# A linear-attention mix: two score levels copied by another engine, more projection products between the scores, and an earlier begin

## The reference

```python
log_a = jax.nn.log_sigmoid(g_in @ w_up + b_up) / 16        # per key channel
# per chunk and head, G = cumsum(log_a)
o_inter = einsum('tk,kv->tv', q_ * exp(G), S)
A[t, s] = sum_k q_[t, k] * k_[s, k] * exp(G[t, k] - G[s, k])   for s <= t
o = o_inter + A @ v_
S = exp(G_last)[..., None] * S + (k_ * exp(G_last - G)).T @ v_
```

## Time and profile before

| | us |
|---|---|
| median of 3 runs | 2460.87 |
| lowest and highest run | 2460.1, 2465.82 |
| span of the profiled execution | 2455.2 |
| TensorE busy | 2293.2 (93%) |
| VectorE, ScalarE, POOL busy | 1172.6, 876.3, 902.2 |

### The profile page before, as it was taken

The page is one execution under the profiler, slowest core; times in us unless marked ns, Lnnn a source line. Parts: engine busy times, 40 slices in busy tenths (PEclk is TensorE's granted clock), DMA queues, the critical chain, the costliest instruction groups (busy, mean ns, idle before and its releaser), DMA issues.

```text
span 2455.2 us, 35075 instructions
## 1 busy us (share of the span) xinstructions
PE 2293.2 (93%) x14164; PEld 1750.4 (71%) x14164; DVE 1172.6 (48%) x2262; ACT 876.3 (36%) x1444; POOL 902.2 (37%) x962
## 2 busy tenths in 40 slices
PE   7988999999999999879999889999999999998898
PEld 7866878986695876545697678789857859664456
DVE  4278243525336127666333881446162452277662
ACT  4332124714334334333333222156143244333341
POOL 2255112215525410555422642122345263115552
PEclk9989999999999999989999999999999999999899
DMA  4100232230100113100321003312301002131003
GB/s 151 56 19 1 87 107 87 70 137 1 35 18 1 50 56 120 60 1 1 138 70 56 19 2 98 121 61 95 112 1 35 18 1 69 37 137 43 1 1 129
DMA packets 92016, 141.28 MB, mean 58 GB/s; under 512 B 18352, under 2 KB 65488, under 8 KB 91856
## 3 DMA queue, kind: packets, MB, share of 16 engines
q1 hardware_dynamic: 91856, 139.05, 16.6%
HBM read 105.48 MB, written 33.55 MB: 57 GB/s over the span
## 4 chain that ended last, share of the span: by engine, by line
PE 79%; DVE 14%; ACT 2%; issue 2%; POOL 2%; DMA 0%; SPq 0%; POOLq 0%; DVEq 0%; ACTq 0%
PE psum L240 37%; PE psum L504 12%; PE psum L1392 5%; PE psum L1354 3%; DVE gla_A L766 3%; PE psum L1375 3%; PE psum L1340 3%; PE psum L1378 3%; PE psum L1380 3%; PE psum L745 2%; PE psum L1399 1%; PE psum L997 1%; POOL w_lo L198 1%; PE psum L1778 1%; PE psum L882 1%
## 5 line engine op out<-in xcount | busy, mean ns | idle before, releaser
L198 POOL TENSOR_TENSOR w_lo<-w_raw,w_hi 128x512 fp32r<-128x512 f32 (+3 forms) x240 | 322.1, 1374 | 823.6 <-ACT w_hi L189 823.6
L240 PE MATMUL psum<-h_hi,w_hi 128*128 128x512 f32 x768 | 200.8, 404 | 0.0
L240 PE MATMUL psum<-h_lo,w_hi 128*128 128x512 f32 x768 | 199.1, 403 | 0.0
L1587 POOL TENSOR_TENSOR mla_acc<-mla_acc,mla_p 128x512 f32<-128x512 f32 (+3 forms) x160 | 159.7, 1015 | 103.1 <-ACT mla_p L1446 103.1
L240 PE MATMUL psum<-h_hi,w_lo 128*128 128x512 f32 x768 | 192.2, 392 | 0.0
L240 PE MATMUL psum<-w_hi,h_hi 128*128 128x256 f32 (+3 forms) x1280 | 183.7, 286 | 0.0
L240 PE MATMUL psum<-w_hi,h_lo 128*128 128x256 f32 (+3 forms) x1280 | 179.6, 283 | 0.0
L240 PE MATMUL psum<-w_lo,h_hi 128*128 128x256 f32 (+3 forms) x1280 | 179.4, 283 | 0.0
L1587 POOL TENSOR_TENSOR fox_acc<-fox_acc,fox_p 128x512 f32<-128x512 f32 (+3 forms) x160 | 149.9, 958 | 75.5 <-ACT fox_p L1446 75.4
L189 ACT ACTIVATE w_hi<-w_raw 128x2048 fp32r<-128x2048 f32 (+3 forms) x60 | 113.6, 1893 | 175.1 <-PE psum L504 169.8
L240 PEld LDWEIGHTS psum<-h_lo,w_hi 128*128 128x128 f32 x768 | 147.7, 195 | 32.1
(11 more groups left out here) (324 smaller groups left out, 4428.8 us busy)
## 6 DMA issues: line engine op xcount, KB each, us to landing
w_raw<-in_w_in_dram SPq DMA_DIRECT2D x38, 1024.0 KB, 5.3
out_dram<-x_rows SPq DMA_DIRECT2D x64, 512.0 KB, 2.7
x_rows<-out_dram SPq DMA_DIRECT2D x56, 512.0 KB, 5.2
w_raw<-in_w_out_dram SPq DMA_DIRECT2D x16, 1024.0 KB, 6.5
x_first<-in_x_dram SPq DMA_DIRECT2D x8, 512.0 KB, 7.0
x_rows<-in_x_dram SPq DMA_DIRECT2D x8, 512.0 KB, 6.0
w_raw<-in_w_in_dram SPq DMA_DIRECT2D x2, 1088.0 KB, 8.7
w_raw<-in_w_in_dram SPq DMA_DIRECT2D x2, 1056.0 KB, 5.2
```

The costliest lines, as they stand in the source:

```text
L198: last = pool.tensor_tensor(self.w_lo[c["set"]][:, at], self.w_raw[c["set"]][:, at], self.w_hi[c["set"]][:, at].bitcast(F32), ALU.subtract)
L240: last = pe.matmul(o, lhs, rhs, start=(kk == 0 and n == 0), stop=(kk == KT - 1 and n == 2))
L1587: pool.tensor_tensor(acc, acc, p, ALU.add).then_inc(self.acc_done.sem, 1)
```

## The change

Three things. (1) In every tile levels 1 and 2 of A are no longer predicated copies of VectorE but plain copies of ScalarE (move_level: one for level 1, on 64 partitions, two for level 2, on 32 each), placed between decay and square; the next batch's scores, finish and the next tile wait for their signal (moved). (2) The slots hold ten matmuls each, 240 in all, which are the two k units of the second half of the positions and the eight dx units, cut where they fall. The mix begins behind the two k units of the first half; tile 4 waits for the others. z stands one unit earlier, ScalarE takes the logs before the third q unit, makes the decays of tile 0 behind the first k unit, and rounds dx0 behind the second. (3) POOL splits dx1 and gA0 by quarters, behind batch 1 and behind the end of tiles 2, 3 and 6, 7.

```diff
     def split_chunk(self, pool, layer, name):
+        for i in range(4):
+            self.split_quarter(pool, layer, name, i)
+    def split_quarter(self, pool, layer, name, i):
         j = self.chunk_of[layer, name]
...
         n = self.chunk_size(c)
-        pool.wait_ge(self.w_rounded, j + 1)
-        for i in range(4):
-            at = slice(i * n // 4, (i + 1) * n // 4)
-            last = pool.tensor_tensor(self.w_lo[c["set"]][:, at], self.w_raw[c["set"]][:, at],
-                                      self.w_hi[c["set"]][:, at].bitcast(F32), ALU.subtract)
-        last.then_inc(self.w_split, 1)
+        if i == 0:
+            pool.wait_ge(self.w_rounded, j + 1)
+        at = slice(i * n // 4, (i + 1) * n // 4)
+        last = pool.tensor_tensor(self.w_lo[c["set"]][:, at], self.w_raw[c["set"]][:, at],
+                                  self.w_hi[c["set"]][:, at].bitcast(F32), ALU.subtract)
+        if i == 3:
+            last.then_inc(self.w_split, 1)
...
     def product(self, pe, layer, name, n, *part):
+        self.product_part(pe, layer, name, n, 0, KT, *part)
+    def product_part(self, pe, layer, name, n, first_kk, end_kk, *part):
...
         w_hi, w_lo = (w[c["set"]][:, :KT * width].rearrange("p (k n) -> p k n", n=width) for w in (self.w_hi, self.w_lo))
-        if n == 0:
+        if n == 0 and first_kk == 0:
             self.wait_bank(pe, u)
-        if n == 0 and first:
+        if n == 0 and first_kk == 0 and first:
             pe.wait_ge(self.w_rounded, j + 1)
...
         w, h = ((w_hi, self.h_hi), (w_hi, self.h_lo), (w_lo, self.h_hi))[n]
-        for kk in range(KT):
+        for kk in range(first_kk, end_kk):
             if c["kind"] == "C":
...
             last = pe.matmul(o, lhs, rhs, start=(kk == 0 and n == 0), stop=(kk == KT - 1 and n == 2))
-        if n == 2:
+        if n == 2 and end_kk == KT:
             last.then_inc(self.unit_done, 1)
...
 C_PARTS = [(m, n) for m in range(2) for n in range(2)]
+BY_HALF = [(m, n) for n in range(2) for m in range(2)]
 OUT_GROUPS = [(h, n) for h in range(2) for n in range(2)]
...
     chunk("q", "C", C_AQ, CHUNK, 0)
-    chunk("k", "C", C_AK, CHUNK, 1)
+    k.add_chunk(layer, "k", "C", C_AK, CHUNK, 1)
+    for part in BY_HALF[:2]:
+        k.add_unit(layer, "k", part, "act")
     k.ring, k.turn = (2, 3), 0
+    for part in BY_HALF[2:]:
+        k.add_unit(layer, "k", part, "act")
     chunk("dx0", "C", C_DX, CHUNK, 0)
...
     IN, END = LEVELS, LEVELS + 1
-    OPS = 1 + LEVELS
+    PLAIN = 2
+    OPS = 1 + LEVELS - PLAIN
     BATCHES = ((1, 2), (3, 4, 5), (6, 7))
...
              "gla_mean": TT, "gla_rstd": TT, "gla_normed": TT, "y_turned": self.GROUPS, "y_ready": self.GROUPS,
-             "end_decays": 1}
+             "end_decays": 1, "gla_moved": TT * self.PLAIN}
         (self.loaded, self.masks_loaded, self.a_turned, self.a_copied, self.z_done, self.z_biased, self.logs, self.exponents,
...
          self.out_done, self.state_product, self.state_new, self.squares, self.mean, self.rstd_ready, self.normed,
-         self.y_turned, self.y_ready, self.end_decays) = (Signal(k, name, count) for name, count in n.items())
+         self.y_turned, self.y_ready, self.end_decays, self.moved) = (Signal(k, name, count) for name, count in n.items())
...
-    def chunk_pool(self, pool, c):
-        if c == 0:
-            self.k.evacuated(pool, self.layer, "k", 1, 1)
+    def chunk_pool(self, pool, c, between):
+        if c in (0, TT // 2):
+            self.k.evacuated(pool, self.layer, "k", 1, 2 * c // TT)
         pool.wait_ge(self.decays.sem, self.decays.at(c + 1))
...
             last.then_inc(self.products.sem, 1)
+            if b == 1:
+                between(pool)
         for slot, src in ((self.IN, self.qT), (self.END, self.kT)):
...
         last.then_inc(self.chunk_ends.sem, 1)
+        between(pool)
...
         if c == 0 and b == 0:
-            self.k.evacuated(pe, self.layer, "k", 1, 1)
+            self.k.evacuated(pe, self.layer, "k", 1, 0)
             pe.wait_ge(self.z_biased.sem, self.z_biased.at(GN * self.N16))
...
             pe.wait_ge(self.masked.sem, self.masked.at(self.OPS * c))
+            pe.wait_ge(self.moved.sem, self.moved.at(self.PLAIN * c))
+            if c == TT // 2:
+                self.k.evacuated(pe, self.layer, "k", 1, 1)
+        elif b == 1:
+            pe.wait_ge(self.moved.sem, self.moved.at(self.PLAIN * (c + 1)))
         else:
-            pe.wait_ge(self.masked.sem, self.masked.at(self.OPS * c + self.BATCHES[b][0]))
+            pe.wait_ge(self.masked.sem, self.masked.at(self.OPS * c + self.BATCHES[b][0] - self.PLAIN))
         if b == 0:
...
         for x, level in enumerate(self.BATCHES[b]):
+            if level <= self.PLAIN:
+                continue
             B = self.HALF >> (level - 1)
-            dve.wait_ge(self.masked.sem, self.masked.at(n0 + level))
+            dve.wait_ge(self.masked.sem, self.masked.at(n0 + level - self.PLAIN))
             ps = self.scores_at(b, x, self.HALF).rearrange("p i g (n b) -> p (i g) n b", b=B)
...
+    def move_level(self, act, c, level):
+        if level == 1:
+            act.wait_ge(self.masked.sem, self.masked.at(self.OPS * c + 1))
+        B = self.HALF >> (level - 1)
+        ps = self.scores_at(0, level - 1, self.HALF).rearrange("p i g x -> p (i g) x")
+        for n in range(self.HALF // B):
+            r, first = slice(2 * B * n, 2 * B * n + B), 2 * B * n + B
+            last = act.activation(self.A[r, :, first:first + B], ps[r, :, B * n:B * n + B], ACT.Copy)
+        last.then_inc(self.moved.sem, 1)
...
             self.decay(act, c + 1)
+        self.move_level(act, c, 1)
+        self.move_level(act, c, 2)
         if c >= 1:
...
         pe.wait_ge(self.masked.sem, self.masked.at(self.OPS * (c + 1)))
+        pe.wait_ge(self.moved.sem, self.moved.at(self.PLAIN * (c + 1)))
         for g in range(GN):
...
             gla.turn_a(pe)
-        if i == 2:
+        if i == 1:
             gla.z(pe)
-    for part in C_PARTS:
+    for part in BY_HALF[:2]:
         k.project(pe, L, "k", *part)
     for c in range(TT):
-        gla.mix_pe(pe, c, lambda pe, n: k.product(pe, L, f"dx{c // 4}", n, *C_PARTS[c % 4]))
+        gla.mix_pe(pe, c, lambda pe, b: units_between(pe, k, L, gla.NBATCH * c + b))
     k.project(pe, L, "gA0", *C_PARTS[0])
...
         a.outA.group(pe, h, n)
+BETWEEN = 10
+UNIT_MATMULS = 3 * KT
+def unit_between(x):
+    if x < 2:
+        return "k", BY_HALF[2 + x]
+    return f"dx{(x - 2) // 4}", C_PARTS[(x - 2) % 4]
+def ended_between(slot):
+    return range(BETWEEN * slot // UNIT_MATMULS, BETWEEN * (slot + 1) // UNIT_MATMULS)
+def units_between(pe, k, layer, slot):
+    at, end = BETWEEN * slot, BETWEEN * (slot + 1)
+    while at < end:
+        x, rest = divmod(at, UNIT_MATMULS)
+        n, kk = divmod(rest, KT)
+        some = min(KT - kk, end - at)
+        name, part = unit_between(x)
+        k.product_part(pe, layer, name, n, kk, kk + some, *part)
+        at += some
...
         act.wait_ge(setup.done.sem, setup.done.at(1))
-    for part in C_PARTS[2:]:
-        gla.evac_qk(act, "q", *part)
+    gla.log_decays(act, link)
+    gla.evac_qk(act, "q", *C_PARTS[2])
+    gla.evac_qk(act, "q", *C_PARTS[3])
+    gla.evac_qk(act, "k", *BY_HALF[0])
+    gla.begin_act(act, link)
+    gla.evac_qk(act, "k", *BY_HALF[1])
     k.round_chunk(act, L, "dx0")
-    gla.log_decays(act, link)
-    for part in C_PARTS:
-        gla.evac_qk(act, "k", *part)
-    gla.begin_act(act, link)
+    def evac_between(slot):
+        for x in ended_between(slot):
+            name, part = unit_between(x)
+            if name == "k":
+                gla.evac_qk(act, "k", *part)
+            else:
+                lru.evac_dx(act, int(name[2:]), *part)
     for c in range(TT):
         if c >= 1:
-            lru.evac_dx(act, (c - 1) // 4, *C_PARTS[(c - 1) % 4])
+            evac_between(3 * c - 2)
+            evac_between(3 * c - 1)
         gla.mix_act(act, link, c)
+        evac_between(3 * c)
         if c == 1:
...
             k.round_chunk(act, L, "gA0")
-    lru.evac_dx(act, 1, *C_PARTS[3])
+    evac_between(3 * TT - 2)
+    evac_between(3 * TT - 1)
     gla.mix_end_act(act, link)
...
             k.split_chunk(pool, L, name)
+        low = iter([("dx1", i) for i in range(4)] + [("gA0", i) for i in range(4)])
         for c in range(TT):
-            gla.chunk_pool(pool, c)
-            if c == 2:
-                k.split_chunk(pool, L, "dx1")
-            if c == 6:
-                k.split_chunk(pool, L, "gA0")
+            gla.chunk_pool(pool, c, lambda pool: k.split_quarter(pool, L, *next(low)) if c in (2, 3, 6, 7) else None)
         for name in ("gA1", "gD0", "outA0"):
...
```

## The result

The changed kernel takes 2440.1 us (median of 4 runs, 2439.4 to 2442.5), the one before 2462.7 (4 runs, 2460.1 to 2465.8): ratio 0.992, 95% interval 0.990 to 0.994. The forecast was 2438.5, range 2424 to 2454.

The account below looks back on a forecast made before the run. TensorE, busy 93%, could win only its gaps in the linear-attention mix. Savings of 11.2 and 10.9 us in the two layers took the span from 2455.2 to 2433.1; plus 5.7 gave 2438.8, rounded 2438.5, range 2424 to 2454.

Parts of the forecast that it names:

- Part 1: Mix slots: ten products instead of eight, taking back 10.9 us of k work; each slot 2.40 us, bounds 2.27 to 2.56.
- Part 2: Levels 1 and 2: ScalarE's three copies take 1.18 us and cost nothing; a quiet tile becomes 15.16 us.
- The slack of 0.1 us: Quiet tile's slot 0: copies let scores start near 7.15 us, just before the slot itself ends at 7.23.
- Part 3: Start of the mix: L745 at 123.6, 6.9 us earlier, after some 8 us idle, losing 4.0; tile 0 takes 13.8.
- Part 4: Quarter splits on VectorE's exponents: stalls of 2.2, 1.6 and 1.5 us, 5.3 a layer, bounds 3.2 to 7.7.
- rival B: Idle stretches of 1.5 to 2.2 us also drop TensorE's clock: 2.3 us a tile, 2452 us; chance 0.13.
- Rival A: Quarters fall into VectorE's waits and cost nothing: 2 x 5.3 us less, 2428 us; chance 0.18.
- C: No change: stalls at their upper bound of 7.7 us and lower clock behind each, 2457 us; chance 0.05.
- D: Slower: ScalarE's copies become the link, slot 0 ending 2.3 us later in every tile, 2475 us; chance 0.06.

Follow-up runs that it names:

- the first experiment: The changed kernel measured again, unaltered, against the kernel before on the same chip: 2441.4 us, ratio 0.993, span 2438.1.
- second: The changed kernel with levels 1 and 2 back on VectorE: 2432.2 us, 9.2 under the changed kernel, ratio 0.990 to the kernel before.
- seventh experiments: The kernel before with only levels 1 and 2 copied by ScalarE: 2464.5 us against 2458.3, ratio 1.001.
- the best kernel: Changed kernel with dx0 rounded behind the fourth q unit, no ScalarE copies, quarters behind batch 1 of tiles 2-7, two more ending tile 7: 2417.2 us, ratio 0.983 to before.

## Why the prediction was right, and where it was lucky

**The median** was met within 1.6 us, but by two errors of opposite sign, and that is luck. The sum was made against a profiled span of 2455.2 and gave 22.1 us; the spans differ by 16.9, and the medians of the first experiment by 16.5. (The 22.5 between the medians of the result comes from four runs of the kernel before that were all slower than its profiled execution.) At the first layer's gA0 8.5 us were won (11.2 forecast), at the second's, 1457.33 instead of 1474.69, 17.4 (22.1). And the step "the median of runs stands 5.7 above the profiled span and I carry that" was wrong: the changed kernel's profiled execution has a span of 2438.3 in a run of 2440.0, so only 1.7 us lie outside the span. The kernel before varies from run to run, and its profiled execution was faster than each run shown.

**Part 1** held. Slots of 2.49 for 2.40 forecast, within its bounds. Alone it brought 6.6 to 9 us (10 expected).

**Part 2** held in quiet tiles: three copies took 1.24 us (195.38 to 196.62 in the quiet tile), forecast 1.18, and cost nothing there. The slack of 0.1 us that the prediction named was the weak point, as the second and seventh experiments showed.

**Part 3** held closely: 123.86 for 123.6, tile 0 13.82 for 13.8. Moving one line showed the cause.

**Part 4** was the mis-sized term. For tile 2 it put 2.2 us. The wait itself was right: slot 0 lasted 4.53 us (157.83 to 162.36) instead of 2.49, 2.0 more. But the lower clock behind it took the rest: 20.40 - 15.25 = 5.2 us in the first layer. Tile 3 cost 0.8 (forecast 1.6) and tile 6, from 220.03 to 236.32, 1.0 (forecast 1.5). The sum over the first layer's mix is 127.3 for 124.8. In the second the same tile took 18.85, 3.6 over a quiet one. So rival B came true in one tile of three; "waits of 0.5 to 0.8 never did it" was correct, and one of 1.97 did. B's own price was short as well: it took the eight products at the 3.15 us of the mix's start, while behind the 3.34 us wait that it names they took 3.78 in the tile of the earlier trace rows (timeline of TensorE, before):

```profile
171.86 3.78 PE L240 MATMUL psum<-h_lo,w_hi 128*128 128x512 f32 x8
```

Rival A fell: quarters do find the exponents. Rivals C and D fell too.

The prediction did not ask what the kernel would be without the copies. It had the two facts needed, VectorE's 1.4 us of slack ahead of the diagonal and ScalarE's 0.1 ahead of the copies, and could have seen that the change undoes part of its own gain.

The second layer's mix begins at 1331.36, where the first layer's 8.5 and the start's 6.9 would make it 1330.6. Nothing is to be read from that 0.8: in the first experiment, an execution of the same kernel, the mixes begin at 125.10 and 1330.25, so 1.2 us later and 1.1 earlier. Left open is why single runs of one kernel spread so widely, 12 us for the kernel before on one chip. The lower clock, which came or stayed away behind the same waits, is one part of it; how large a part isn't shown.

## What to carry to other kernels

Before moving work to an engine with idle time, look at what stands in front of it in that engine's queue when it falls due: ScalarE was busy 37% and still the later of the two. Shared-resource work (POOL's passes beside VectorE's) is cheap where the other engine waits and dear on its critical passes, so cut it and place it by the timeline. When work is pulled forward, follow every in-order queue that feeds its first instruction; here one rounding in the wrong place was worth 11.7 us by the spans and 15.7 by the medians.

## What was not expected of the hardware

An exponent on VectorE takes as long as the POOL instruction beside it, whichever that is: 0.60 us beside one of 0.56, 0.81 beside one of 0.77, 1.35 beside 1.31, and 0.28 alone. The Trainium skill (SBUF — State Buffer, Who interferes with whom) has this as an exclusive lock for the whole instruction; the rows agree. Small products are the milder neighbours, though. Alone, exponents start every 0.20 us; beside products of 0.56 us they start every 0.53, beside a quarter 1.28 us apart. So a microsecond of such products delays VectorE by some 0.6 us, one of quarters by some 0.8 (estimates from the rows of VectorE in tile 2).

The granted clock: in the two executions of the changed kernel each layer had an idle stretch of 1.91 or 1.97 us in tile 2, and each time TensorE ran at 1.2 GHz for part of the tile, at a mean of 0.83 once and 0.91 three times. Behind waits of 0.93 us (tile 6) and 0.88 us the 48 scores took their full-clock 1.57. But the length of a wait alone doesn't settle it: the best kernel had waits of 0.69 and 1.05 us ahead of tile 0 in both layers, and the clock fell in one (13.08 us, mean 0.87) and not in the other (11.98 us, 1.00). The same code paid 20.40 and 18.83 us for the same wait, so such a stall should be priced with a margin, not with its idle time.
